# Modulation folds and Fourier channel products as products of 64 output partitions or 64 contracted rows, issued in turns

## What is computed

```python
cond_lat = jax.nn.silu(c)
cond_ctx = jax.nn.silu(c_ctx)
mod = (cond_lat @ w_ada[layer] + b_ada[layer]).reshape(x.shape[0], N_MOD, 1, D_MODEL)
mod_c = (cond_ctx @ w_ada[layer] + b_ada[layer]).reshape(N_MOD, 1, D_MODEL)
...
def fourier_mix(u):
    b, l, _ = u.shape
    g = u.astype(jnp.float32).reshape(b, l, FOURIER_GROUPS, FOURIER_GROUP_DIM)
    y = jnp.fft.fft2(g, axes=(1, 3), norm='ortho').real
    return y.reshape(b, l, FOURIER_WIDTH).astype(u.dtype)
```

## Time and profile before

| | |
|---|---|
| median of 3 runs | 2784.86 us (2778.41 to 2785.48) |
| the profiled execution | 2781.14 us |
| its span, first to last instruction | 2779.0 us |
| PE busy in matmuls | 2692.2 us, 97% of the span, 15515 records |
| DVE busy | 1540.4 us, 55% |
| ACT busy | 697.0 us, 25% |
| chain of work that ended last | PE 91%, DVE 4%, ACT 2% |
| mean granted clock of TensorE | 0.987 of full |

### The profile page before, as it was taken

One profiled execution on the slowest core, in us unless ns is written; L12 is line 12 of the kernel. 1 busy time (PEld: TensorE's weight loads), 2 busy tenths in 40 slices (PEclk: granted clock), 3 DMA queues, 4 the chain that ended last, 5 costly groups with the idle time before them and its releaser, 6 DMA issues.

```text
span 2779.0 us, 42188 instructions
## 1 busy us (share of the span) xinstructions
PE 2692.2 (97%) x15515; PEld 2331.0 (84%) x15515; DVE 1540.4 (55%) x2701; ACT 697.0 (25%) x1075; POOL 49.1 (2%) x51
## 2 busy tenths in 40 slices
PE   6999999999989999999999999999999989999998
PEld 4888888888879888888888888888887869888886
DVE  5776477543368377626773677257535466533332
ACT  4111111132247231111111311111113245422222
POOL 0000000000021000000000000000000020000000
PEclk9999999999989999999999999999999999999999
DMA  7877477413200167626762577257422300233332
GB/s 223 194 184 182 112 182 186 118 51 83 61 1 2 46 144 186 164 63 163 185 162 60 125 183 172 70 144 185 121 67 72 83 16 7 80 96 106 91 103 86
DMA packets 485789, 316.89 MB, mean 114 GB/s; under 512 B 30588, under 2 KB 483664, under 8 KB 485712
## 3 DMA queue, kind: packets, MB, share of 16 engines
q1 hardware_dynamic: 485712, 315.88, 44.5%
HBM read 313.73 MB, written 2.10 MB: 114 GB/s over the span
## 4 chain that ended last, share of the span: by engine, by line
PE 91%; DVE 4%; ACT 2%; issue 1%; DMA 1%; SPq 1%; DVEq 0%; ACTq 0%
PE pg L647 79%; PE pg L714 4%; PE p L951 2%; PE pn L935 1%; PE p L662 1%; DVE xlo L1480 1%; PE pg L894 1%; DVE tnorm L1472 1%; ACT whi L1043 0%; PE pg L899 0%; DMA ada_first<-in_w_ada 0%; DVE wlo L1332 0%; ACT qd L1148 0%; PE pg L900 0%; ACT xhi L1115 0%
## 5 line engine op out<-in xcount | busy, mean ns | idle before, releaser
L647 PE MATMUL pg<-xhi,whi 128*128 128x512 f32 x2880 | 801.9, 347 | 8.2 <-DVE wlo L1332 6.2
L647 PE MATMUL pg<-xlo,whi 128*128 128x512 f32 x2880 | 797.7, 345 | 0.0
L647 PE MATMUL pg<-xhi,wlo 128*128 128x512 f32 x2880 | 797.0, 345 | 0.0
L1043 ACT CAST whi<-raw 128x1024 fp32r<-128x1024 f32 (+1 forms) x288 | 321.7, 1118 | 1072.6 <-PE pg L647 1065.2
L1332 DVE TENSOR_TENSOR wlo<-raw,whi 128x1024 fp32r<-128x1024 f32 (+1 forms) x288 | 377.6, 1311 | 349.2 <-ACT whi L1043 346.3
L647 PEld LDWEIGHTS pg<-xhi,whi 128*128 128x128 f32 x2880 | 455.5, 188 | 77.8 <-DVE wlo L1332 7.7
L647 PEld LDWEIGHTS pg<-xhi,wlo 128*128 128x128 f32 x2880 | 456.1, 188 | 70.5
L647 PEld LDWEIGHTS pg<-xlo,whi 128*128 128x128 f32 x2880 | 455.6, 188 | 69.5
L1413 DVE SCALAR_TENSOR_TENSOR part<-ada,cond,part 128x256 f32<-128x256 f32 x960 | 465.3, 485 | 32.7
L1521 DVE SCALAR_TENSOR_TENSOR h<-pg,gcol,h 128x512 f32 (+1 forms) x118 | 71.4, 639 | 452.9 <-PE pg L647 452.9
L647 PE MATMUL pg<-ahi,whi 128*128 128x512 f32 x1100 | 305.9, 346 | 0.0
(11 more groups left out here) (202 smaller groups left out, 2017.3 us busy)
## 6 DMA issues: line engine op xcount, KB each, us to landing
ada<-in_w_ada SPq DMA_DIRECT2D x512, 256.0 KB, 4.1
raw<-in_ffn_w_in SPq DMA_DIRECT2D x176, 512.0 KB, 3.9
raw<-in_ffn_w_out SPq DMA_DIRECT2D x64, 704.0 KB, 4.5
raw<-in_w_in SPq DMA_DIRECT2D x24, 512.0 KB, 4.0
ada_first<-in_w_ada SPq DMA_DIRECT2D x8, 1024.0 KB, 12.0
raw<-in_w_in SPq DMA_DIRECT2D x16, 256.0 KB, 3.6
raw<-in_w_o SPq DMA_DIRECT2D x16, 256.0 KB, 2.7
raw<-in_w_o SPq DMA_DIRECT2D x32, 128.0 KB, 2.9
```

The lines of the kernel that those rows point to most:

```text
L647: last = nc.tensor.matmul(pg[s][:, p0:p1], w[:, s, k], v[:, k, p0:p1], start=(k == 0 and n == 0), stop=(k == kt - 1 and n == 2))
L1043: nc.scalar.copy(whi[:, s, 0:nk], raw[:, s, 0:nk]).then_inc(s_whi[s], 1)
```

## The change

In `ada_fold` each product with 128 output partitions becomes two with 64: columns 0 to 63 of the tile of `part` go to output partitions 0 to 63, columns 64 to 127 to output partitions 64 to 127, one after the other, so that the four products of a fold alternate between the halves.

In the Fourier stage each product with 128 contracted rows and 256 columns becomes two with 64 contracted rows and 128 columns, on the upper and lower half of the partitions in turns. The half b of the channels goes to the bank b of a PSUM tensor of two banks: `p67` for even blocks, `pn` for odd blocks. Both banks of `p67` now belong to one block. The zeros of `cs64` are no longer read. The copies to `pq` read the two banks with a pattern (256 columns of each) and write `pq` in the old layout through `pq_blocks`.

```diff
--- before.py
+++ after.py
@@ -443,6 +443,10 @@
+        def pq_blocks(tt):
+
+            return pq[:, tt].rearrange("p (c b d) -> p c b d", c=4, b=2)
+
         turn_order = [4, 5, 0, 3, 1, 2]
         fwd, bwd = [4, 5, 0, 1, 2, 3], [5, 4, 3, 2, 1, 0]
 
@@ -659,8 +663,11 @@
                 pe.wait_ge(s_sum, sum_value(t, i) + ADA_TILES)
                 pe.wait_ge(s_mod, i + t // 2)
                 for b in range(2):
-                    last = nc.tensor.matmul(pa[1][:, 2 * b:2 * b + 2], part[:, b * P:(b + 1) * P], halves,
-                                            start=True, stop=True)
+                    for h in range(2):
+                        own = slice(HD * h, HD * h + HD)
+                        last = nc.tensor.matmul(pa[1][own, 2 * b:2 * b + 2],
+                                                part[:, b * P + HD * h:b * P + HD * h + HD], halves,
+                                                start=True, stop=True)
                 last.then_inc(s_fold, 1)
 
 
@@ -782,8 +789,12 @@
                     if tt >= 2:
                         pe.wait_ge(s_pq[l][tt % 2], tt // 2)
                     for ft in range(2):
-                        last = nc.tensor.matmul(pa[tt % 2][:, ft * 256:ft * 256 + 256],
-                                                z[:, F_T + ft, tt * P:(tt + 1) * P], cs64, start=True, stop=True)
+                        for b in range(2):
+                            own, at = slice(HD * b, HD * b + HD), 512 * b + ft * P
+                            last = nc.tensor.matmul((p67, pn)[tt % 2][:, at:at + P],
+                                                    z[own, F_T + ft, tt * P:(tt + 1) * P],
+                                                    cs64[own, :].rearrange("p (c d) -> p c d", c=2)[:, :, own],
+                                                    start=True, stop=True)
                     last.then_inc(s_f1[l], 1)
 
                 for b in range(2):
@@ -1178,7 +1189,8 @@
                 for tt in range(0, nt, 2):
                     act.wait_ge(s_f1[l], tt + 1)
                     length = SEQ if tt < SEQ // P else CTX
-                    nc.scalar.mul(pq[:, tt], pa[0], float((length * HD) ** -0.5)).then_inc(s_pq[l][0], 1)
+                    nc.scalar.mul(pq_blocks(tt), p67[:, :].rearrange("p (b q) -> p b q", b=2)[:, :, 0:256].rearrange(
+                        "p b (c d) -> p c b d", d=HD), float((length * HD) ** -0.5)).then_inc(s_pq[l][0], 1)
                 for dr in range(2):
                     b = (2 * l + dr) * RH
                     nc.scalar.activation(kdec[:, :, dr], lg[:, b:b + RH], ACT.Exp, scale=kpos[:, dr:dr + 1])
@@ -1611,7 +1623,8 @@
                 for tt in range(1, nt, 2):
                     dve.wait_ge(s_f1[l], tt + 1)
                     length = SEQ if tt < SEQ // P else CTX
-                    nc.vector.tensor_scalar(pq[:, tt], pa[1], float((length * HD) ** -0.5), None, ALU.mult
+                    nc.vector.tensor_scalar(pq_blocks(tt), pn[:, :].rearrange("p (b q) -> p b q", b=2)[:, :, 0:256].rearrange(
+                        "p b (c d) -> p c b d", d=HD), float((length * HD) ** -0.5), None, ALU.mult
                                             ).then_inc(s_pq[l][1], 1)
                 decay_args()
                 query_decay(0)
```

## The result

| | before | after |
|---|---|---|
| median of the runs | 2784.51 us (2778.41 to 2785.48, 4 runs) | 2810.70 us (2808.31 to 2813.52, 4 runs) |
| profiled execution: span | 2779.0 us | 2806.3 us |
| mean granted clock of TensorE | 0.987 | 0.987 |

The ratio is 1.0105, with an interval of 1.0089 to 1.0120: the change makes the kernel slower by about 26 us. The forecast was 2789 with a range of 2778 to 2798, so the time lies outside it, on a side to which 0.17 had been given. The two profiled spans differ by 27.3 us.

What follows compares the result with a forecast made beforehand. TensorE, busy 97% of the span, was taken as the bound, its chain mostly weight products. Folds +5.8 us and Fourier -1.4 gave +4.4 on the 2784.86 median: 2789 us, range 2778 to 2798.

Steps and rivals of the forecast that it cites:

- The fold: Modulation fold among the weight products: 0.54 us on PE against 0.45, +0.09 us, times 64 = +5.8 us.
- Entering: Step into the fold behind a 256-column product: 0.12 us streaming plus 0.09 lost, so first load about 0.21 later.
- the change of shape costs nothing: Rival at the fold: loads still hide, fold takes 0.24, 14.8 us saved with Fourier, 2770; chance 0.12.
- it costs 0.15 each way: Rival at the fold: each shape change costs 0.15, fold 0.66 us, +12 in all, 2797; chance 0.12.
- the halves follow each other: Rival at the fold: eight loads in a row, fold 0.78 us, +19.7 with Fourier, 2805; chance 0.08.
- in the fold's new order: Mixing-stage lines 863 and 865, taken to alternate halves like the new fold and show loads in pairs.
- The Fourier term: Fourier products of both mixing stages, split into 64 rows and 128 columns: together -1.4 us.
- the fourth rival: Clock halves in Fourier stage: 1.4 us gone or a loss up to 1; 2791 to 2792; chance 0.08.
- layer 0's 0.83: Layer 0's Fourier stage: block 4's copy, and with it ACT's run of copies, comes 0.83 us earlier.
- layer 1's 0.6: Layer 1's Fourier stage: ACT's dec comes 0.6 us earlier in all.
- The upper end of the range: 2798 us, made from the rival in which each change of shape at the fold costs 0.15.

Runs made afterwards that it cites:

- fold_serial: Kernel before with the half-width fold, both products of the lower output half first, then both of the upper; 2815.59 us (one run).
- fourier_only: Kernel before with only the Fourier stage of the change, folds as before; 2783.22 us, ratio 0.9994.
- fourier_lead: Kernel before with the Fourier split and idle two-column products ahead of six loops without folds, old fold kept; 2778.29 us, ratio 0.9982.
- fold_only: Kernel before with only the new fold of the change, Fourier stage as before; 2811.65 us, ratio 1.0095.
- new_fold_full1: Kernel before with the half-width fold and one unread full-width two-column product behind each fold; 2815.18 us, ratio 1.0108.
- old_fold_n132: Kernel before with its full-width fold given 132 moving columns where 2 are needed; 2790.14 us (one run).
- new_fold_full2: Kernel before with the half-width fold and two unread full-width two-column products behind each fold; 2830.83 us (one run).
- n34: Kernel before with the half-width fold given 34 moving columns instead of 2 in every pass; 2804.19 us (one run).
- n66: Kernel before with the half-width fold given 66 moving columns instead of 2 in every pass; 2806.70 us (one run).
- n132: Kernel before with the half-width fold given 132 moving columns instead of 2 in every pass; 2832.05 us (one run).
- full2_lead_in: Half-width fold with two full-width two-column products behind it, plus idle lead-in products also ahead of the loops with folds; 2830.40 us (one run).
- lead_in: Kernel before with two full-width two-column products, results unread, ahead of six loops without folds; 2783.15 us, ratio 0.9987.

## Why the prediction failed

**The fold: right.** Entering 0.20 (forecast 0.21), pairs of loads at 0.05 to 0.06, the whole 0.53 (0.54), 64 times +0.079 us. The rivals that disputed it are out: that the change of shape costs nothing, that it costs 0.15 each way (0.66 a fold), and that the halves follow each other (0.78). The loads of the two column halves, which share all rows, start 0.006 us apart, and fold_serial costs only 0.01 us more. One reading beneath it was wrong and did no harm: lines 863 and 865 are not "in the fold's new order" but go two products to one half and then two to the other, the order of fold_serial. The rule of the Trainium skill, "TensorE: Matmul & The Clock Gate", Part 3, that a load overlaps matmuls in flight only when its row group differs, is not borne out by the fold either.

**The Fourier term: right in mechanism at full clock, too large in every run.** The copies kept their length on both engines. But the fourth rival, which had been given 0.08, is what mostly happened: the clock fell ahead of the last of the stage's products in both layers of fourier_only and fourier_lead and in layer 0 of the kernel after, in five stages of six, and in none of the 32 such stages of the 16 kernels with the old form. Only layer 1 of the kernel after kept full clock through its products, and there 0.57 came of the 0.6. Of layer 0's 0.83 came 0.71 in fourier_lead, where the clock fell last, 0.30 in fourier_only and -0.08 in the kernel after; of layer 1's 0.6 came 0.14 in fourier_only and 0.04 in fourier_lead. Instead of 1.4 us dec came earlier by 0.49 (after), 0.44 (fourier_only) and 0.75 (fourier_lead) over both layers. In the kernel before the clock was down from 776.8 for 6.8 us behind layer 0's stage, and over the whole span it was down for 73.7 us before and for 73.6 after; fourier_only and fourier_lead had 97.1 and 80.0, but with one profile each that can be chance.

**The step that failed is one that the prediction never wrote down**: that the stream of weight products, with the time it takes for a pair, is the same behind the new fold as behind the old. It says that "what PE spends or saves between two of those products goes straight into the end", and counts only what lies between. The sum lacked a term, 4888 pairs x 4.92 ns = +24.0 us, four times the one that it had. With it the sum is 5.1 + 24.0 - 0.5 = 28.6 us of span, and 27.3 was measured. The upper end of the range had been made from a larger fold alone, so it could not hold it.

The trace of the kernel before held the warning. The earlier trace rows were read as "a 512 and a 256 together take 0.35", which hides the two values, and the fold was judged by the gap around it. Between 68.5 and 85.1 us, ahead of the first fold, that kernel runs at 353.3, behind it at 346.7; the loops at 636, 1453 and 1740 us run at 353.3. Of the folds themselves five turned 353.3 into 346.7, every one that met it, and three went the other way. So the old fold was worth something that no row of its own shows: it set the stream right or kept it so, 61 times.

**What stays open** is the cause inside PE. Shown: the pace depends on how the stream is re-entered; more moving columns that lengthen the mean fold by only 6 to 8 ns are enough to change it (0.543 us never led to 346.7, 0.551 did in a part of the program; the old fold at 0.462 alternates, at 0.456 it did not), though the length alone does not decide, since single folds of the kernel before take 0.450 or 0.456 and both have 346.7 behind; a fold may lead nearly always to one pace (before; the new fold of after and fold_only too, but in only one of 128 cases from the faster), exchange the two (new_fold_full1, old_fold_n132), or keep them (new_fold_full2); and neither an emptied array, nor halves, nor a full-width load ahead of the stream decides it by itself. Only argued, and in no run shown, is that loads and products can lock in two or more relative positions, since a 256-column product streams for hardly longer (0.12 us) than a load of 128 columns takes (the old fold's loads stand 0.11 apart), and that the slower one leaves a load waiting for a few cycles once a pair. I could not say in advance which pace a given fold would leave behind: of the runs that tried, n34 and n66 changed it in places that nothing had pointed to, n132 not at all, and full2_lead_in in other parts than expected.

## What to carry to other kernels

Where one stream of matmuls fills most of the time, measure its pace from start to start over many products, separately for every stretch between interruptions, before pricing an edit inside it: two values that differ by 2% are worth more than the edit. A small insert in such a stream is then judged not by its own gap alone but by the stretch behind it, and a forecast for a changed insert needs the other pace as a case with its price (here 24 us), even when nothing says how likely it is. Shorter loads in an insert are no gain if the stream restarts worse behind them. A couple of idle products in front of a loop may be worth their cost, but must be tried in the kernel at hand: in lead_in six of six loops took the faster pace, in full2_lead_in four of nine. And halving the work of a stage in which PE waits can bring the half clock into it, which here took back 0.7 to 1.0 us of a gain of 1.4.

## What the runs showed of the hardware

- Alternating float32r products of 512 and 256 columns, each with its own load, run at 346.7 or at 353.3 ns a pair at full clock; loops with 512 columns alone ran at 226.7 ns a product before and after, with no second value seen.
- A product of 64 output partitions behind full width costs 0.09 us beyond the stream on the way in, as much as on the way out, also between a 256-column product and one with two columns.
- Loads of the two column halves start 0.006 us apart although they share all rows, 0.013 when they are not issued in turns; the order of the halves makes 0.01 us a fold.
- The granted clock fell in five of six Fourier stages in the new form (PE busy 1.38 of 3.40 us ahead of it in the kernel after), and in none of 32 in the old form.
- A wait of PE for its own last product costs 0.75 us at a loop's end, much more than a change of shape (0.09).
- Reading two banks with gaps costs neither ACT (0.60 us for 512 columns) nor DVE (0.68 to 0.69) anything.
